# Two-layer hybrid decoder trunk on one core: openings with x normalised on ScalarE, transposes inside the output stage, and a first block whose adaptive tiles are used as they land

## The chip, the cores and the metric

The kernel runs on one core of a Trainium2 chip. The metric is the device time in microseconds (us) of one execution; lower is better. TensorE is called PE below, VectorE DVE, ScalarE ACT, GpSimd POOL, and the DMA queue that SyncE feeds SP. All data is fp32. A weight or an activation that enters a large product is first split into two fp32r parts, a high part (a rounding copy, on ACT) and a low part (the subtraction, on DVE or POOL), and a product is three matmuls.

## The reference

Each of two layers applies three sub-layers to x (512 tokens, 1024 channels): a SwiGLU FFN with half weight, a token mixer with four branches, and a second FFN. Around each sits the same frame:

```
def rmsnorm(x, g):
    y = xf * lax.rsqrt(jnp.mean(xf * xf, axis=-1, keepdims=True) + EPS)
    return (y * g.astype(jnp.float32)).astype(x.dtype)

def sandwich(x, y_fn, g_pre, g_post, shift, scale, gate, resid_w):
    h = rmsnorm(x, g_pre) * (1.0 + scale) + shift
    return x + resid_w * gate * rmsnorm(y_fn(h), g_post)

def swiglu(h, w_in, w_out):
    gate, up = jnp.split(h @ w_in, 2, axis=-1)
    return (jax.nn.silu(gate) * up) @ w_out

mod = (jax.nn.silu(c) @ w_ada[l] + b_ada[l]).reshape(B, 9, 1, D_MODEL)
```

shift, scale and gate are slices of `mod`, the "adaptive" vectors; they come from `w_ada`, 9 x 1024 x 1024 numbers a layer. The first sub-layer of layer 0 needs two of the nine slices (shift and scale) before anything else can begin.

## The kernel before, in words

**Weights** come as a stream of units of 512 KB (128 x 1024 fp32). Four slots hold them. For each unit SP loads `w_raw`, ACT makes `w_high` (`split_high`, L436), DVE makes `w_low` (`split_low`, L442), and PE uses it (`product`, L458 to L460, with the weights stationary and h moving; `token_product`, L465 to L467, in the output stage, with the activations stationary).

**Output stage** (`out_stage`, L1404). Its second half works token block by token block (tb 0 to 3, 128 tokens each): for each tb the last four units are run through, and a token block's result is complete after every 24 matmuls of 512 columns.

**Closing** (L848 on ACT, L1241 on DVE, L589 on POOL). For each tb: ACT sums the squares of y, DVE makes the mean, POOL takes the power -1/2, DVE adds y to x in two halves (L1253), ACT sums the squares of the new x (L845), DVE makes their mean (`mean_x`), and POOL makes the reciprocal root and from it a diagonal matrix `rstd_diag` (`rstd_diag`, L580).

**Opening** (L1447 on PE, L1266 on DVE, L866 on ACT). h must be channel-major. PE multiplies x by the diagonal matrix (`h_block`, L1449), which normalises and transposes at once, 8 matmuls of 128x128 for a token block, into banks 4 to 7. Then for each pair of token blocks and each of 8 channel tiles j, DVE applies scale and shift (`h_full`, L1286), ACT makes `h_high` (L873), DVE makes `h_low` (L1274). PE multiplies tile by tile into three units' banks (`products`, L1458): 8 tiles x 3 units x 3 matmuls of 256 columns for each pair. Both token blocks of pair 0 are transposed before the first product, those of pair 1 after the sixth tile of pair 0.

There are six openings: five follow an output stage, and are called boundaries below; the first has no stage before it. Before the first, SP loads the silu input, constants, 16 rows of adaptive weights in eight transfers of 1 MB (`ada_start`), three weight units after the fourth of these, then x (2 MB). DVE takes one product sum of 1024 for each of the 16 rows (L1324): eight shift rows, the low parts of three units, eight scale rows. Then `vec_scale` is made for all channels at once.

After an opening that starts an FFN, DVE increments `ada_free`; SP waits for that before it issues the silu vector, the next weight units and the adaptive tiles of the FFN, in this order in one queue. DVE needs the first adaptive tile before it completes the first FFN pair, which PE waits for after the fourth unit.

The order on each engine is the order of the code: there is no scheduler. Each engine runs its queue in order, and a wait holds all that is behind it.

## Time and profile before

| | us |
|---|---|
| median of 3 runs | 2825.34 |
| lowest, highest | 2823.95, 2826.14 |
| time of the profiled execution | 2821.51 |
| its span, first to last instruction | 2819.7 |
| PE busy | 2731.5 (97%) |
| DVE busy | 1563.4 (55%) |
| ACT busy | 1108.9 (39%) |
| POOL busy | 269.1 (10%) |

The profile was taken in one execution. 1.8 us lie around its span. PE is busy for 97% of the span, so the time outside PE's work is 88 us, and 36 us of that is the start. The mean granted TensorE clock was 0.998 of full speed.

### The profile page before, as it was taken

To read this page: it belongs to the slowest core of one execution; us is meant where nothing else is said; L and a number is where in the kernel's file an instruction comes from. 1 tells how busy PE (TensorE), PEld (TensorE's weight loads), DVE (VectorE), ACT (ScalarE), POOL (GpSimd) and SP (SyncE) were. 2 spreads that over 40 slices of the span, in tenths; PEclk is the share of its full clock that TensorE was granted. 3 is DMA by queue.
4 is the path that set the end of the run, shared out by engine and by line. 5 is a ranking of instruction groups with operands and counts; after the bars stand their busy time and mean duration, and the time that the engine had idled before them with its cause. 6 is when DMAs were issued, how large, how long until landed. Compare 5 with 4: busy or idle time off the path is not lost.

```text
span 2819.7 us, 37695 instructions
## 1 busy us (share of the span) xinstructions
PE 2731.5 (97%) x13312; PEld 2205.2 (78%) x13312; DVE 1563.4 (55%) x2636; ACT 1108.9 (39%) x2024; POOL 269.1 (10%) x360
## 2 busy tenths in 40 slices
PE   4999999999999999999999999999999999999999
PEld 4888888676777888888888888877667778888887
DVE  6655446657755657633266653565577465653323
ACT  2322234665554443222242222346665443332222
POOL 1111000111110001110011110001111000011100
PEclk9999999999999999999999999999999999999999
DMA  6655422111223325523235544221122223152331
GB/s 235 234 181 196 142 99 75 61 53 61 68 61 98 98 73 194 194 97 97 98 120 208 193 150 156 90 77 54 52 62 74 86 72 106 52 193 97 97 97 68
DMA packets 86253, 318.55 MB, mean 113 GB/s; under 512 B 9697, under 2 KB 10081, under 8 KB 84706
## 3 DMA queue, kind: packets, MB, share of 16 engines
q1 hardware_dynamic: 86114, 316.76, 33.0%
q8 instruction: 79, 1.29, 0.2%
q14 instruction: 60, 0.49, 0.1%
HBM read 314.62 MB, written 2.10 MB: 112 GB/s over the span
## 4 chain that ended last, share of the span: by engine, by line
PE 86%; DVE 6%; ACT 2%; DVEq 2%; issue 2%; DMA 2%; SPq 0%; POOL 0%; ACTq 0%; POOLq 0%
PE bank L458 19%; PE bank L460 19%; PE bank L459 19%; PE bank L465 6%; PE bank L466 6%; PE bank L467 6%; PE bank L1686 2%; PE bank L1667 2%; PE bank L1650 1%; DVE w_low L442 1%; PE bank L1658 1%; DMA ada_raw<-ada 1%; ACT w_high L436 1%; PE bank L1453 1%; DVEq L973 1%
## 5 line engine op out<-in xcount | busy, mean ns | idle before, releaser
L458 PE MATMUL bank<-h_high,w_high 128*128 128x512 f32 (+1 forms) x2528 | 974.5, 385 | 20.7 <-DVE h_low L1274 12.4
L460 PE MATMUL bank<-h_high,w_low 128*128 128x512 f32 (+1 forms) x2528 | 956.9, 379 | 0.0
L459 PE MATMUL bank<-h_low,w_high 128*128 128x512 f32 (+1 forms) x2528 | 955.3, 378 | 0.0
L442 DVE TENSOR_TENSOR w_low<-w_raw,w_high 128x1024 fp32r<-128x1024 f32 x437 | 565.7, 1296 | 634.7 <-ACT w_high L436 633.3
L436 ACT ACTIVATE w_high<-w_raw 128x1024 fp32r<-128x1024 f32 x437 | 458.5, 1051 | 357.0 <-PE bank L467 331.6
L458 PEld LDWEIGHTS bank<-h_high,w_high 128*128 128x128 f32 x2528 | 478.1, 189 | 114.2 <-issue 30.7
L460 PEld LDWEIGHTS bank<-h_high,w_low 128*128 128x128 f32 x2528 | 476.9, 189 | 90.2
L459 PEld LDWEIGHTS bank<-h_low,w_high 128*128 128x128 f32 x2528 | 477.9, 189 | 86.4 <-issue 2.4
L465 PE MATMUL bank<-w_high,ffn_high 128*128 128x512 f32 x704 | 275.6, 391 | 0.0
L467 PE MATMUL bank<-w_low,ffn_high 128*128 128x512 f32 x704 | 273.9, 389 | 0.0
L466 PE MATMUL bank<-w_high,ffn_low 128*128 128x512 f32 x704 | 273.9, 389 | 0.0
L908 ACT ACTIVATE ffn_high<-ffn_act 128x512 f32 (+1 forms) x88 | 55.7, 632 | 417.0 <-DVE ffn_act L1368 417.0
L616 POOL TENSOR_TENSOR ffn_low<-ffn_act,ffn_high 128x512 f32 x88 | 114.0, 1295 | 879.8 <-ACT ffn_high L908 879.8
L603 POOL TENSOR_TENSOR recip<-row_sum,parv 128x1 f32<-128x1 f32 x192 | 106.8, 556 | 648.1 <-ACT scores_sb L789 648.1
L1297 DVE CUSTOM_DVE_ANT_0 ada_raw<-ada_raw,silu_c 128x1024 f32<-128x1024 f32 x128 | 154.6, 1215 | 10.5 <-DMA ada_raw<-ada 10.5
L465 PEld LDWEIGHTS bank<-w_high,ffn_high 128*128 128x128 f32 x704 | 132.2, 188 | 28.4 <-issue 1.0
L466 PEld LDWEIGHTS bank<-w_high,ffn_low 128*128 128x128 f32 x704 | 132.2, 188 | 28.0 <-issue 1.0
L467 PEld LDWEIGHTS bank<-w_low,ffn_high 128*128 128x128 f32 x704 | 132.1, 188 | 27.7
L904 ACT ACTIVATE tanh_gate<-bank 128x512 f32<-128x512 f32 x88 | 52.4, 595 | 227.5 <-PE bank L460 227.5
L1368 DVE TENSOR_TENSOR ffn_act<-ffn_act,bank 128x512 f32<-128x512 f32 x88 | 60.5, 687 | 130.5 <-PE bank L460 129.1
L789 ACT ACTIVATE scores_sb<-scores_sb,neg_max 128x257 f32<-128x257 f32 (+5 forms) x192 | 101.8, 530 | 75.2 <-DVE neg_max L1157 74.5
L774 ACT ACTIVATE probs_t<-bank 128x256 f32<-128x256 f32 (+3 forms) x192 | 77.8, 405 | 133.0 <-PE bank L1667 131.9
(194 smaller groups left out, 2698.9 us busy)
## 6 DMA issues: line engine op xcount, KB each, us to landing
w_raw<-stream SPq DMA_DIRECT2D x440, 512.0 KB, 3.6
ada_raw<-ada SPq DMA_DIRECT2D x128, 512.0 KB, 3.5
ada_start<-ada SPq DMA_DIRECT2D x8, 1024.0 KB, 17.0
mixer_consts<-mixc SPq DMA_DIRECT2D x2, 1152.0 KB, 5.1
x<-x_in SPq DMA_DIRECT2D x1, 2048.0 KB, 18.8
silu_c<-silu_row SPq DMA_DIRECT2D x4, 512.0 KB, 4.3
out<-x SPq DMA_DIRECT2D x8, 256.0 KB, 2.1
lru_w<-lruw SPq DMA_DIRECT2D x2, 512.0 KB, 4.0
```

The lines of the kernel that those rows point to most:

```text
L436: eng.activation(wH[:, slot], raw[:, slot], ACT.Copy).then_inc(hi_ready[slot].sem, 1)
L442: eng.tensor_tensor(wL[:, slot], raw[:, slot], wH[:, slot].bitcast(F32), ALU.subtract).then_inc(lo_ready[slot].sem, 1)
L458: eng.matmul(o, a, rhs_h, start=first, stop=False)
L459: eng.matmul(o, a, rhs_l, start=False, stop=False)
L460: return eng.matmul(o, b, rhs_h, start=False, stop=last)
L465: eng.matmul(o, lhs_h, a, start=first, stop=False)
L466: eng.matmul(o, lhs_l, a, start=False, stop=False)
L467: return eng.matmul(o, lhs_h, b, start=False, stop=last)
L603: pool.tensor_tensor(recip[:, g % 8:g % 8 + 1], rsum[:, c:c + 1], mone, ALU.pow).then_inc(recip_ready.sem, 1)
L616: pool.tensor_tensor(fL[:, m, :], act[:, pp:pp + 1, :], fH[:, m, :].bitcast(F32), ALU.subtract).then_inc(ffn_lo.sem, 1)
L789: s.activation(s_sb[:, g % S_SLOTS, 0:w], s_sb[:, g % S_SLOTS, 0:w], ACT.Exp, scale=-1.0, bias=nmax[:, c:c + 1], accum_out=rsum[:, c:c + 1 ...
L1297: v.tensor_tensor_reduce(row, row, silu_c[:, :], 1.0, 0.0, ALU.mult, ALU.add, mod_sum[:, s:s + 1]).then_inc(ada_used.sem, 1)
```

## The change

Three things change in the five boundaries. First, normalising and transposing are separate: ACT multiplies x by the reciprocal root (`x_norm`, new L912, two activations of 512 a token block) and PE does a plain transpose against the identity. Second, the transposes of token blocks 0 and 1 stand inside the output stage, after the second of the four last units of tb 2 and of tb 3. Third, closing and opening are one function, `boundary`, in which the work of both is interleaved: on DVE the first tiles of h stand before the last token block's new x; POOL makes the low part of one weight unit (instead of DVE) and of every odd h tile.

The first opening is a function of its own. x is loaded before the adaptive tiles, whose layout is changed: for each channel tile j there is one row for the shift (a DVE product sum as before) and one 128 x 1024 tile for the scale, which PE multiplies by the silu column (`scale_row`, 8 matmuls with one moving column each). x is normalised on ACT as a whole, and PE makes products of 512 columns tile by tile as the adaptive tiles land. `ones` and `all_par` are loaded last.

```diff
-            rows = 2 * KD // ADA_GROUPS
-            for g in range(ADA_GROUPS):
-                sp.dma_start(ada_start[:, rows * g:rows * (g + 1)], ada0[:, rows * g:rows * (g + 1)]
-                             ).then_inc(ada_start_in[g].sem, 16)
-                if g == ADA_GROUPS // 2 - 1:
+            sp.dma_start(x[:, :, :], x_in).then_inc(x_loaded.sem, 16)
+            for g in range(KD):
+                sp.dma_start(ada_start[:, 2 * g:2 * g + 2], ada0[:, 2 * g:2 * g + 2]).then_inc(ada_start_in[g].sem, 16)
+                if g == 0:
                     for u in range(LEAD):
                         sp.dma_start(raw[:, u], stream[u]).then_inc(raw_full[u].sem, 16)
-                    sp.dma_start(x[:, :, :], x_in).then_inc(x_loaded.sem, 16)
             sp.dma_start(raw[:, LEAD], stream[LEAD]).then_inc(raw_full[LEAD].sem, 16)
+            sp.dma_start(ones[:, :], consts[:, P:2 * P]).then_inc(late_in.sem, 16)
+            sp.dma_start(all_par[:, :, :], pars).then_inc(late_in.sem, 16)
...
+            def boundary(l, n, u_last):            # POOL
+                for tb in range(TB - 1):
+                    rstd_y(l, n, tb)
+                    if tb < 2:
+                        rstd_x(l, n, tb)
+                split_low(pool, l, u_last + 1)
+                h_low_odd(l, n, 1)
+                rstd_x(l, n, 2)
+                h_low_odd(l, n, 3)
+                rstd_y(l, n, 3)
+                h_low_odd(l, n, 5)
+                rstd_x(l, n, 3)
+                for i in range(7, 2 * KD, 2):
+                    h_low_odd(l, n, i)
...
+            def boundary(l, n, u_last):            # ACT
+                for tb in range(TB - 1):
+                    squares_y(l, n, tb, u_last)
                     if tb == 2:
                         split_high(s, l, u_last + 1)
+                    squares_of_x(l, n, tb)
+                    if tb < 2:
+                        x_norm(l, n, tb)
+                split_high(s, l, u_last + 2)
+                h_high(l, n, 0)
+                h_high(l, n, 1)
+                split_high(s, l, u_last + 3)
+                squares_y(l, n, 3, u_last)
+                x_norm(l, n, 2)
+                h_high(l, n, 2)
+                h_high(l, n, 3)
+                squares_of_x(l, n, 3)
+                for i in range(4, KD):
+                    h_high(l, n, i)
+                x_norm(l, n, 3)
+                split_high(s, l, u_last + 4)
+                for i in range(KD, 2 * KD):
+                    h_high(l, n, i)
...
+            def boundary(l, n, u_last):            # DVE
+                for tb in range(TB - 1):
+                    new_x(l, n, tb)
+                    if tb < 2:
+                        mean_x(l, n, tb)
+                two(0)
+                split_low(v, l, u_last + 2)
+                mean_x(l, n, 2)
+                split_low(v, l, u_last + 3)
+                two(2)
                 v.drain()
+                new_x(l, n, 3)
+                two(4)
+                mean_x(l, n, 3)
+                two(6)
+                split_low(v, l, u_last + 4)
+                for i in range(KD, 2 * KD, 2):
+                    two(i)
...
+            for j in range(KD):                    # DVE, first opening
+                v.wait_ge(ada_start_in[j].sem, 16)
+                v.tensor_tensor_reduce(ada_start[:, 2 * j], ada_start[:, 2 * j], silu_start[:, :], 1.0, parv[:, j:j + 1],
+                                       ALU.mult, ALU.add, mod[:, 7 * KD + j:7 * KD + j + 1])
+                v.drain()
+                v.wait_ge(start_scale.sem, j + 1)
+                v.scalar_tensor_tensor(vecA[:, j:j + 1], bank[3][:, j:j + 1], b1[:, j:j + 1],
+                                       parv[:, 2 * KD + j:2 * KD + j + 1], ALU.add, ALU.mult).then_inc(start_vec.sem, 1)
+                if j == 1:
                     for u in range(LEAD):
+                        split_low(v, 0, u)
+                if j >= 1:
+                    start_low(j - 1)
+            start_low(KD - 1)
+            split_low(v, 0, LEAD)
...
+                    if q == units - RING + 1 and tb >= 2 and not ends(l, n):   # PE, output stage
+                        h_block(pe, l, n, tb - 2)
...
+            slots = []                                                          # PE, opening
+            for j in range(LEAD):
+                slots.append(unit_ready(pe, l, u_first + j))
+                for k in range(2):
+                    if j == 0:
+                        h_wait(0, k)
+                    unit_product(0, k, j, slots[j])
+            for k in range(2, KD - 2):
                 products(0, k)
+            h_block(pe, l, n, 2)
+            products(0, KD - 2)
+            h_block(pe, l, n, 3)
+            products(0, KD - 1)
             for k in range(KD):
                 products(1, k)
...
+            for k in range(KD):                                                 # PE, first opening
+                if k + 1 < KD:
+                    scale_row(k + 1)
+                if 4 <= k + 3 < KD:
+                    x_tile(k + 3)
+                pe.wait_ge(start_h.sem, k + 1)
```

`two(i)` on DVE writes the h tiles i and i + 1 and then the low part of tile i; POOL makes that of tile i + 1. Tile i + 1 needs the second half of the double buffer, so it waits for POOL's low part of tile i - 1 (`h_ready_odd`).

On POOL, around the last two token blocks of a boundary, the kernel before has reciprocal roots and diagonal matrices only (`wi` holds the statistics of y, `row_sum` those of x):

```order
L594 TENSOR_TENSOR wi<-wi,minus_half 128x1 [waits msy_ready]
L584 TENSOR_TENSOR row_sum<-row_sum,minus_half 128x1 [waits msx_ready]
L586 TENSOR_TENSOR rstd_diag<-ident,row_sum 128x128 [waits rsx_ready]
L594 TENSOR_TENSOR wi<-wi,minus_half 128x1 [waits msy_ready]
L584 TENSOR_TENSOR row_sum<-row_sum,minus_half 128x1 [waits msx_ready]
```

In the same place POOL now has:

```order
L607 TENSOR_TENSOR wi<-wi,minus_half 128x1 [waits msy_ready]
L458 TENSOR_TENSOR w_low<-w_raw,w_high 128x1024 [waits hi_ready2]
L620 TENSOR_TENSOR h_low<-h_full,h_high 128x256 [waits h_high_ready]
L613 TENSOR_TENSOR row_sum<-row_sum,minus_half 128x1 [waits msx_ready]
L620 TENSOR_TENSOR h_low<-h_full,h_high 128x256 [waits h_high_ready]
L607 TENSOR_TENSOR wi<-wi,minus_half 128x1 [waits msy_ready]
```

The roots of token blocks 2 and 3 now stand behind a weight split and behind low parts of h.

On DVE, from the new x of token block 2 (`y_gain`, `x`) on, the kernel before has three weight splits and the last new x before the first h tile:

```order
L442 TENSOR_TENSOR w_low<-w_raw,w_high 128x1024 [waits hi_ready2]
L442 TENSOR_TENSOR w_low<-w_raw,w_high 128x1024 [waits hi_ready3]
L442 TENSOR_TENSOR w_low<-w_raw,w_high 128x1024 [waits hi_ready0]
...
L1253 SCALAR_TENSOR_TENSOR x<-y_gain,wi,x 128x512 [waits rsy_ready]
...
L1286 TENSOR_SCALAR h_full<-bank,vec_scale,mod 128x256 [waits h_t_ready]
...
L1274 TENSOR_TENSOR h_low<-h_full,h_high 128x256 [waits h_high_ready]
```

There DVE now has (two `h_full`, one `h_low`, then two splits, two `h_full`, one `h_low`, and only then the last new x):

```order
L1358 TENSOR_SCALAR h_full<-bank,vec_scale,mod 128x256 [waits h_t_ready]
L1363 TENSOR_TENSOR h_low<-h_full,h_high 128x256 [waits h_high_ready]
L458 TENSOR_TENSOR w_low<-w_raw,w_high 128x1024 [waits hi_ready3]
...
L458 TENSOR_TENSOR w_low<-w_raw,w_high 128x1024 [waits hi_ready0]
...
L1358 TENSOR_SCALAR h_full<-bank,vec_scale,mod 128x256 [waits h_ready_odd]
...
L1340 SCALAR_TENSOR_TENSOR x<-y_gain,wi,x 128x512 [waits rsy_ready]
```

Four h tiles of pair 0 are made before the last new x, and four after it.

On PE, in the first opening, the kernel before has 16 scaled transposes and then products. PE now has, from the second adaptive tile on (`recip` is the silu column, `x_start` the normalised x):

```order
L1615 MATMUL bank<-recip,ada_start 128x1 [waits start_vectors,ada_start_in2]
L1615 MATMUL bank<-recip,ada_start 128x1 x7
L1623 MATMUL bank<-ident,x_start 128x128 [waits start_h_full]
L1623 MATMUL bank<-ident,x_start 128x128 x3
L474 MATMUL bank<-h_high,w_high 128x512 [waits start_h]
L475 MATMUL bank<-h_low,w_high 128x512
L476 MATMUL bank<-h_high,w_low 128x512
```

The scale tile k + 1 stands in PE's queue before the products of tile k.

## Rows read from the trace of the kernel before

**Rows 1.** The page's head.
```profile
span 2819.7 us, 37695 instructions
```

**Rows 2.** Waits of PE: who was waited for; total us, times, longest.
```profile
PE bank L1453 <- POOL rstd_diag L586: 35.8, 1, 35.8
PE bank L458 <- DVE h_low L1274: 12.4, 6, 2.5
PE bank L458 <- DVE ffn_act L1368: 5.3, 4, 2.2
```

**Rows 3.** Timeline of the start: start, duration, engine, line, operation [idle before].
```profile
19.17 1.06 ACT L885 ACTIVATE w_high<-w_raw 128x1024 fp32r<-128x1024 f32 x1 [12.68 <-DMA w_raw<-stream]
...
26.67 0.63 ACT L845 ACTIVATE squares_out<-x 128x512 bf16<-128x512 f32 x1 [3.88 <-DMA x<-x_in]
...
29.10 1.28 DVE L1324 CUSTOM_DVE_ANT_0 ada_start<-ada_start,silu_start,parv 128x1024 f32<-128x1024 f32 x1 [5.07 <-DMA ada_start<-ada]
...
35.75 5.81 PE L1453 MATMUL bank<-rstd_diag,x 128*128 128x128 f32 x32 [35.75 <-POOL rstd_diag L586]
...
42.71 0.36 PE L458 MATMUL bank<-h_high,w_high 128*128 128x256 f32 x1 [1.15 <-DVE h_low L1274]
```

**Rows 4.** Timeline of PE in the mixer, one-column matmuls.
```profile
446.24 2.84 PE L1511 MATMUL bank<-ones,squares 128*128 128x1 f32 x24 [1.21 <-ACT squares L718]
```

**Rows 5.** Chain of waits: start, length, what; a product of 512 columns.
```profile
406.30 0.23 PE bank L466
```

**Rows 6.** Chain of waits, in the same columns, a product in an opening.
```profile
423.06 0.12 PE bank L458
```

**Rows 7.** Chain of waits, four transposes in the mixer.
```profile
600.70 0.44 PE bank L1667 x4
```

**Rows 8.** Timeline of PE at the first boundary.
```profile
410.67 3.73 PE L1453 MATMUL bank<-rstd_diag,x 128*128 128x128 f32 x32
416.58 0.36 PE L458 MATMUL bank<-h_high,w_high 128*128 128x256 f32 x1 [2.18 <-DVE h_low L1274]
...
423.25 3.79 PE L1453 MATMUL bank<-rstd_diag,x 128*128 128x128 f32 x32
...
437.56 0.28 PE L460 MATMUL bank<-h_high,w_low 128*128 128x256 f32 x1
```

**Rows 9.** Timeline of DVE at the same boundary.
```profile
410.15 2.56 DVE L442 TENSOR_TENSOR w_low<-w_raw,w_high 128x1024 fp32r<-128x1024 f32 x2 [0.30 <-ACT w_high L436]
...
413.47 1.42 DVE L1253 SCALAR_TENSOR_TENSOR x<-y_gain,wi,x 128x512 f32<-128x512 f32 x2
414.98 0.99 DVE L1286 TENSOR_SCALAR h_full<-bank,vec_scale,mod 128x256 f32<-128x256 f32 x2
416.01 0.43 DVE L1274 TENSOR_TENSOR h_low<-h_full,h_high 128x256 fp32r<-128x256 f32 x1
...
433.24 0.43 DVE L1274 TENSOR_TENSOR h_low<-h_full,h_high 128x256 fp32r<-128x256 f32 x1
```

**Rows 10.** Timeline of ACT at the same boundary.
```profile
415.56 0.87 ACT L873 ACTIVATE h_high<-h_full 128x256 fp32r<-128x256 f32 x2
```

**Rows 11.** Timeline of POOL at the same boundary.
```profile
404.87 0.40 POOL L586 TENSOR_TENSOR rstd_diag<-ident,row_sum 128x128 f32<-128x128 f32 x1
...
410.56 1.08 POOL L586 TENSOR_TENSOR rstd_diag<-ident,row_sum 128x128 f32<-128x128 f32 x1
412.86 0.55 POOL L594 TENSOR_TENSOR wi<-wi,minus_half 128x1 f32<-128x1 f32 x1 [1.23 <-DVE wi L1246]
```

**Rows 12.** The line of POOL's subtraction of 512: ns min/median/max.
```profile
L616 POOL TENSOR_TENSOR ffn_low<-ffn_act,ffn_high x88: 1287/1296/1303, 72.2 to 2694.5; 128x512 f32 x88
```

**Rows 13.** Timeline of SP after the first opening.
```profile
59.76 0.35 SPq L527 DMA_DIRECT2D silu_c<-silu_row  x1
```

**Rows 14.** Timeline of PE, the first product after the fourth unit.
```profile
71.48 0.49 PE L458 MATMUL bank<-h_high,w_high 128*128 128x512 f32 x1 [2.24 <-DVE ffn_act L1368]
```

**Rows 15.** Busy time by windows at the third boundary: PE, PEld, DVE, ACT, POOL, granted clock.
```profile
1432.00:1436.00 4.00, 4.00 (x22) 3.91 (x21) 3.62 (x9) 1.78 (x5) 0.38 (x1) 0.57 0.00 0
```

More of the change, by code:

```diff
@@ L619, in _ @@
                         turn(i)
-                    closing(l, 2 * f)
+                    if ends(l, 2 * f):
+                        for tb in range(TB):
+                            rstd_y(l, 2 * f, tb)
+                    else:
+                        boundary(l, 2 * f, U_FFN[f] + FFN_UNITS - 1)
                     if f == 0:
@@ L1713, in _ @@
                     pe.wait_ge(pair_done.sem, pair_done.at(l, f * FT))
-                    opening(pe, l, 1 if f else -1, [u0 + j for j in range(LEAD)])
+                    if f == 1:
+                        opening(pe, l, 1, u0)
+                    elif l > 0:
+                        opening(pe, l - 1, 2, UNITS)
                     turn(0, range(LEAD, 4))
```

359 lines of the change are left out of this document (204 added, 155 removed).

## The prediction

> **What bounds the kernel now.** I read the page first: the span is 2819.7 us [rows 1] and PE is busy in 97% of it, so only PE's own work and its gaps count. The waits of PE come next [rows 2]: 35.8 us before the first matmul, 12.4 us in six waits for `h_low` (one in each opening), and 5.3 us in four waits for the first FFN pair (one after each opening that starts an FFN). Then the timeline of one boundary. With 0 as the end of the last product of the output stage (410.67), PE does 32 records of scaled transposes (3.73), idles to 5.9, does 54 products, 32 more records (3.79 with its tail, 3.55 to the next product) and 90 products, the last of which starts at 26.9; with 0.12 for it the boundary costs PE 27.0 us [rows 6, 8]. DVE finishes the last low part at 23.0 [rows 9], so `ada_free` comes 4 us before PE is through.
>
> **A boundary after the change: PE's work.** 144 products x 0.12 = 17.3 [rows 6]. A plain transpose is one record, four take 0.44 [rows 7], so 32 take 3.5; four switches between kinds at an estimated 0.1 make 3.9. Together 21.2, against 24.4 without the old waits. If nothing waited, a boundary would win 5.8 us. So the question is what waits.
>
> **The waits.** Two facts price them. POOL subtracts 512 columns in 1.296 and scales 128 in 0.40 [rows 11, 12], which by a straight line gives 0.7 for 256 and 2.45 for 1024. And POOL and DVE exclude each other: a POOL instruction that takes 0.40 alone took 1.08 when it began under a DVE subtraction at 410.56; the first of the two splits ended at about 411.38, and 0.26 later POOL was through [rows 9, 11]. So POOL work that meets a DVE subtraction waits for its end, and the other way round.
>
> Let 0 be the end of the last product of the output stage again. Token blocks 0 and 1 are normalised in time: from a finished block to `x_norm` is some 6.5 us, against 8 us and more to its transposes, so both hide. y of block 2 is finished at -6.35. Its new x ends at -3.2. POOL's weight split may begin at -3.7 but is held to -3.2 by DVE's new x, and ends at -0.8. DVE makes h tiles 0 and 1 by -2.2; ACT, which stands at the second unit's high part until -1.3, makes their high parts by -0.5; low part 0 is ready at -0.5. DVE then takes the split of unit 2 to 0.65, and POOL's low part 1 waits behind it to 1.2. PE waits 0.9 for tile 1. The third unit is split by 2.5; PE waits another 0.2 before it. The root for block 2 meets this split and ends at 2.9 (0.55 alone, [rows 11]); ACT's `x_norm` of block 2 runs to 4.1, and the high parts of tiles 2 and 3 stand behind it. With 0.42 to 0.45 for each high and low part [rows 9, 10] and 0.14 from DVE to PE (416.44 to 416.58), tile 2 reaches PE at 5.0: a wait of 1.6. Only now comes the last new x: DVE needs the product with the gain (0.7), POOL's root stands behind low part 3 and ends at 6.3, the additions take 1.42 [rows 9] to 7.7, ACT squares both halves to 8.5, and tile 4 reaches PE at 9.5, where tile 3 was through at 7.2: a wait of 2.3. Tiles 5 to 7 are in time, but block 3's `x_norm` waits until block 2's transposes have left its buffer: 0.4. After it ACT splits a unit (1.06), DVE does (1.23), and only then is tile 8 made: PE gets it at 17.75, a wait of 1.65. From there PE is the slower one (1.08 a tile against 1.8 for two on DVE and POOL) and ends at 26.4.
>
> Waits: 0.9 + 0.2 + 1.6 + 2.3 + 0.4 + 1.65 = about 7, where before they were 2.2 to 2.5. 26.4 and 2.0 for the two blocks of transposes in the output stage make 28.4, against 27.0: **1.4 slower a boundary**. Without any exclusion I get 27.2. DVE and POOL end at 23.9 + 2.0 = 25.9 instead of 23.0, so `ada_free` is 2.9 later. In all four FFN openings PE already waits for what follows `ada_free` [rows 2], so there the later of the two counts: 2.9 for the three boundaries that lead to an FFN, 1.4 for the two that lead to a mixer. Sum 3 x 2.9 + 2 x 1.4 = 11.5.
>
> **The first opening.** A 512 KB unit landed at 19.17, and x, 3 MB later, at 26.67 [rows 3]: 2.45 us a MB. x stands 2.5 MB earlier than the first unit did (4.5 MB of large transfers then, 2 MB now, issued 0.5 us sooner), so it lands at about 12.5, the adaptive tiles 0 to 7 at 14.9, 21.0 and then every 2.45 to 35.6. Squares on ACT and DVE (two blocks each, 1.3 a block) end at 15.3. POOL's power of 128x4 is not shown: above 0.55 for one column, below four times that; I take 1.4, so 17.0. `x_norm` of four times 1.0 ends at 21.0, three high parts at 24. PE's 16 transposes end at 24, scale row 1 at 26.2. DVE then makes three low parts (3.7) before low part 0: 31.0.
>
> From here PE sets the pace. Scale tile k + 1 stands before the products of tile k. One such row is 8 matmuls of fp32, two records each; 24 records of the same form (128x128 stationary, one moving column) took 2.84 [rows 4], so 16 take 1.9. They load 128x128 weights for a single column. Per tile: 1.9 for the scale row, 0.2 to DVE, 0.1 for the vector, 0.7 for the 512-column low part (between 0.43 for 256 and 1.23 for 1024), 0.14 to PE, 9 x 0.23 = 2.05 for the products [rows 5]: 5.1, the transposes lying in DVE's part. That is twice the 2.45 of a landing, so the transfers don't bound it. Six of these bring low part 6 to 61.6; after one more pair of ACT passes, the last low part is ready at 63, the fourth unit's at 64.5, `ada_free` at 64.9. The first matmuls in the old kernel ran slowly: 32 records in 5.8 where a later opening needs 3.7 [rows 3, 8], 2.1 more, a little of it perhaps for POOL's diagonals. PE is idle for 5 us before 31.0, so I charge 1.7: `ada_free` at 66.6, 6.9 later than 59.7 [rows 13]. PE resumed 11.8 after it [rows 14], and I keep that. So the first opening costs **+6.9**; from both sides, -4 if a scale row cost nothing (rival 2) and +9 if all low parts met a slow clock.
>
> **Sum.** 11.5 + 6.9 = +18.4, from 2821.5 for the profiled execution to 2840; the median of the runs lies 3.8 higher, so 2843. All other work is the same: the 1.23 that POOL takes from DVE is off PE's path, and steady loops are untouched.
>
> **The rivals.**
>
> 1. *Waits as forecast, but the clock falls too.* At the third boundary the granted clock was 0.57 over four microseconds after an idle stretch of 2.5 [rows 2, 15], between its levels of 2.4 and 1.2 GHz; that cost 0.43 x 4 = 1.7 us. In the changed boundaries PE waits five times instead of once, and the first opening has a wait in each tile. If four more boundaries fall once (6.8) and the first opening twice more (3.4), the time is 2853. Against it: at the first boundary 2.2 of idle time was followed by 54 products in 6.67 us, 0.12 each [rows 8], so no clock fell there. The Trainium skill ("TensorE: Matmul & The Clock Gate", section "HAM oscillation — how this bites in real kernels") states that matmul groups parted by waits can each start at the lower clock again. By that rule alone this rival would be likelier than the trace makes it.
>
> 2. *Faster: the waits fold into one and scale rows are cheap.* If POOL and DVE overlap more freely and ACT is never the one in front, a boundary has 21.2 + 2.2 = 23.4, which is 3.6 faster, 18 in all; if the one-column matmuls pipeline so that a row costs 0.3, a tile costs 3.4, `ada_free` comes at 56 and 4 are won. Together 2803. For it: half of the transposes' records go, and the output stage has 5 us of lead for two of four blocks. Against it: rows 4 and 11 show both costs directly. The sign turns where the waits of a boundary stay well under 5.8 and a scale row well under 1.0.
>
> 3. *No change.* The saved transposes (3.6 a boundary) are just paid back by waits (about 5.8 in all rather than 7), and the first opening gives -1 to +4, because the low parts run at full clock and x lands sooner than I say: 2822 to 2830, say 2826.
>
> **How the numbers follow.** Forecast 2843: 0.55. Rival 1, 2853: 0.16. Rival 2, 2803: 0.14. Rival 3, 2826: 0.15. 0.2% is 5.65 us, about what a measurement of this kernel tells from no change: faster means below 2819.7, slower above 2831. The forecast's own spread is 2832 to 2852 (1.5 a boundary and 3 for the start). Slower has 0.55 + 0.16 and a little of rival 3, 0.73; within, 0.13; faster, 0.14. The range 2822 to 2857 leaves out rival 2 and a slow tail, 0.14 + 0.04.
>
> **What would show it.** Right: in a boundary PE has about six gaps, of 0.9, 1.6, 2.3 and 1.65 at the tiles 1, 2, 4 and 8; POOL's 256-column subtractions take 0.7 alone and more under DVE; first products start near 31, one tile every 5.1, and SP issues the silu vector near 66. Wrong: gaps of under 4 us a boundary, scale rows of under 1 us, or `ada_free` before 60.

## The result and the profile after

The changed kernel takes 2866.24 us (2862.29 to 2867.11), where the kernel before took 2824.64 on the same chip: a ratio of 1.0141, 95% interval 1.0129 to 1.0153. The forecast was 2843. The direction was right; the loss is 41.6 us instead of 18, and lies outside the range.

First the head of the page of the changed kernel, against [rows 1].

```profile
span 2863.8 us, 37384 instructions
PE 2755.9 (96%) x13176; PEld 2215.4 (77%) x13176; DVE 1543.2 (54%) x2558; ACT 1140.9 (40%) x2057; POOL 303.1 (11%) x378
```

PE has 136 records fewer than before and is busy for longer (2755.9 against 2731.5), at a mean granted clock of 0.989 instead of 0.998. Part of the loss is thus PE running slowly, not PE waiting. Next, the waits of PE after the change, in the columns of [rows 2].

```profile
PE bank L474 <- DVE h_low L1363: 28.6, 17, 2.1
PE bank L1615 <- DMA ada_start<-ada: 14.1, 1, 14.1
PE bank L474 <- DVE ffn_act L1475: 12.5, 4, 3.9
PE bank L474 <- DVE h_low L1419: 7.8, 7, 4.3
PE bank L474 <- POOL h_low L620: 5.0, 5, 1.0
```

The start wait of 35.8 is now 14.1, but inside the boundaries 11.2 us in five waits (the 12.4 of [rows 2] less the 1.15 of the first opening) have become 28.6 and 5.0 in 22, and the four waits for `ffn_act` have grown from 5.3 to 12.5. I measured every stretch from one landmark that both kernels have, ACT's squares of token block 0 of the closing. "To PE's end" is the last 256-column product of the opening, "to SP" the issue of `silu_c`, which follows DVE's end:

| us | before | after |
|---|---|---|
| `silu_c` after the first opening | 59.76 | 72.14 |
| five boundaries, to PE's end | 43.01, 43.00, 44.81, 43.00, 43.00 | 48.57, 47.00, 46.99, 46.99, 47.34 |
| the three that lead to an FFN, to SP | 39.18, 41.00, 39.19 | 44.75, 45.06, 45.10 |

The first opening accounts for 12.4, the two boundaries into a mixer for 5.56 + 3.99, the three into an FFN for 5.57 + 4.06 + 5.91 (by SP, since PE waits there for what follows it). That is 37.5 of the 44.1 by which the span grew. The other 6.6 lie in no boundary. Over the eight microseconds around the end of each wait for `ffn_act` (from 82, 1109, 1491 and 2516) the granted clock is 0.79, where it is 1.00 in the same places before (from 70, 1087, 1461 and 2475): 4 x 8 x 0.21 = 6.7, which is about the whole of it.

**The first boundary.** PE's gaps and transposes of the changed kernel, from its timeline (start, duration, what, idle time before), against [rows 8]:

```profile
428.44 0.35 PE L474 MATMUL bank<-h_high,w_high 128*128 128x256 f32 x1 [2.13 <-DVE h_low L1363]
430.06 0.39 PE L474 MATMUL bank<-h_high,w_high 128*128 128x256 f32 x1 [1.04 <-POOL h_low L620]
433.82 0.39 PE L474 MATMUL bank<-h_high,w_high 128*128 128x256 f32 x1 [1.55 <-DVE h_low L1363]
438.14 0.39 PE L474 MATMUL bank<-h_high,w_high 128*128 128x256 f32 x1 [1.90 <-DVE h_low L1363]
...
444.41 1.09 PE L1567 MATMUL bank<-ident,x_norm 128*128 128x128 f32 x8 [0.41 <-ACT x_norm L912]
448.17 0.39 PE L474 MATMUL bank<-h_high,w_high 128*128 128x256 f32 x1 [1.60 <-DVE h_low L1363]
```

The gaps at tiles 1, 2, 4, 8 and at block 3's transposes are close to those of the forecast (0.9, 1.6, 2.3, 1.65, 0.4). The first one, 2.13 ahead of tile 0, was forecast as nothing. What is late is visible on DVE and POOL, against [rows 9, 11]; first DVE, then POOL:

```profile
422.26 3.57 DVE L1340 SCALAR_TENSOR_TENSOR x<-y_gain,wi,x 128x512 f32<-128x512 f32 x2
425.75 0.99 DVE L1358 TENSOR_SCALAR h_full<-bank,vec_scale,mod 128x256 f32<-128x256 f32 x2
427.87 0.42 DVE L1363 TENSOR_TENSOR h_low<-h_full,h_high 128x256 fp32r<-128x256 f32 x1 [1.13 <-ACT h_high L920]
```

```profile
422.54 2.73 POOL L458 TENSOR_TENSOR w_low<-w_raw,w_high 128x1024 fp32r<-128x1024 f32 x1 [0.35 <-ACT w_high L452]
428.22 1.79 POOL L620 TENSOR_TENSOR h_low<-h_full,h_high 128x256 fp32r<-128x256 f32 x1 [2.94 <-ACT h_high L920]
430.18 1.46 POOL L613 TENSOR_TENSOR row_sum<-row_sum,minus_half 128x1 f32<-128x1 f32 x1 [0.17 <-DVE row_sum L1326]
```

The two additions to x took 1.42 before [rows 9] and take 3.57 now. POOL's split arrives at 422.54, while the first addition is running; it works when that one is done (at about 422.97), and the second addition ends only 0.56 after POOL is through (425.27). So DVE held POOL back for 0.4 at most, and POOL then held DVE for 2.1. That POOL waited for the first addition shows in the first boundary of e_scale_dve (an experiment told below), where the split arrived 0.14 behind the start of the additions (399.22) instead of 0.28 behind it, took 0.13 longer and ended as long after that start, 3.0:

```profile
399.36 2.86 POOL L458 TENSOR_TENSOR w_low<-w_raw,w_high 128x1024 fp32r<-128x1024 f32 x1 [0.21 <-ACT w_high L452]
```

At 428.22 the roles are the other way round: POOL's low part, 0.73 alone, takes 1.79 under DVE's weight split.

**The first opening.** PE's first work in the changed kernel, its timeline:

```profile
14.09 3.54 PE L1615 MATMUL bank<-recip,ada_start 128*128 128x1 f32 x16 [14.09 <-DMA ada_start<-ada]
20.75 3.68 PE L1623 MATMUL bank<-ident,x_start 128*128 128x128 f32 x16 [3.11 <-ACT x_start L964]
24.21 3.41 PE L1615 MATMUL bank<-recip,ada_start 128*128 128x1 f32 x16
```

DVE's side of it, the first and third low part and the vector ahead of the third, in the same columns:

```profile
31.20 0.69 DVE L1419 TENSOR_TENSOR h_low<-norm_tmp,h_high 128x512 fp32r<-128x512 f32 x1
...
44.22 0.22 DVE L1426 SCALAR_TENSOR_TENSOR vec_scale<-bank,mod_sum,parv 128x1 f32<-128x1 f32 x1 [4.48 <-PE bank L1615]
44.35 0.68 DVE L1419 TENSOR_TENSOR h_low<-norm_tmp,h_high 128x512 fp32r<-128x512 f32 x1
```

Low part 0 starts at 31.20, as forecast (31.0). The next ones start at 37.84, 44.35, 50.87, 55.79, 60.75, 67.83 and 69.52: 6.5 to 7.1 us apart where the clock was low, 4.9 where it was full. DVE waits for PE in each, 4.5 to 5.1 in the steps at the low clock and 2.9 in those at full clock. PE stands there at the nine products of the tile before and then at its scale row. Nine products take 2.2 at full clock (51.60 to 53.78) and 3.9 at the lower one (31.94 to 35.83); a row takes 1.84 and 3.4. In this profile it was mostly the products that were slow: of the six rows in these steps one ran at the lower clock throughout:

```profile
58.73 1.84 PE L1615 MATMUL bank<-recip,ada_start 128*128 128x1 f32 x16
64.25 3.41 PE L1615 MATMUL bank<-recip,ada_start 128*128 128x1 f32 x16
```

### The profile page after: what moved, and what is told of

Its sections match the earlier page's. It is cut to its first block, busy times and chain, and to the rows that moved or that the text cites. A ratio compares the mean times of both kernels' runs of the same rounds, so it can differ in the third digit from the quotient of the medians.

```text
span 2863.8 us, 37384 instructions
## 1 busy us (share of the span) xinstructions
PE 2755.9 (96%) x13176; PEld 2215.4 (77%) x13176; DVE 1543.2 (54%) x2558; ACT 1140.9 (40%) x2057; POOL 303.1 (11%) x378
## 4 chain that ended last, share of the span: by engine, by line
PE 82%; DVE 7%; ACT 4%; issue 2%; DVEq 2%; POOL 1%; DMA 1%; ACTq 0%; SPq 0%; POOLq 0%
PE bank L474 19%; PE bank L476 19%; PE bank L475 19%; PE bank L481 6%; PE bank L482 6%; PE bank L483 6%; PE bank L1851 2%; PE bank L1832 2%; PE bank L1815 1%; DVE w_low L458 1%; PE bank L1823 1%; DVE x L1340 1%; DMA ada_raw<-ada 1%; ACT squares_out L889 1%; ACT w_high L452 1%
## 5 line engine op out<-in xcount | busy, mean ns | idle before, releaser
L474 PE MATMUL bank<-h_high,w_high 128*128 128x512 f32 (+1 forms) x2504 | 982.3, 392 | 57.2 <-DVE h_low L1363 28.6
L483 PEld LDWEIGHTS bank<-w_low,ffn_high 128*128 128x128 f32 x704 | 132.1, 188 | 27.6
```

The costliest lines, as they stand in the source:

```text
L474: eng.matmul(o, a, rhs_h, start=first, stop=False)
L483: return eng.matmul(o, lhs_h, b, start=False, stop=last)
```

## The experiments

All ratios are against the kernel before, run beside the experiment on the same chip. The medians come from several chips, on which the kernel before took 2824.0 to 2827.5, so two experiments are compared by their ratios.

**The two halves apart.** The kernel before with the changed first opening alone:

```diff
+            pe.wait_ge(consts_in.sem, 16 * 4)
+            first_opening(pe)
+            pe.wait_ge(late_in.sem, 32)
...
-                    opening(pe, l, 1 if f else -1, [u0 + j for j in range(LEAD)])
+                    if f == 1 or l > 0:
+                        opening(pe, l, 1 if f else -1, [u0 + j for j in range(LEAD)])
```

> The kernel before with the first opening of the changed one; its five boundaries are those of before. Theory (the two parts cost by themselves and add): the silu vector is issued at 72 instead of 59.8, and 1 to 2 us more are lost at the lower clock behind it, so +13 to +15 over before, 2838 to 2840. Rival (the first opening only looks late, since the layer's loads make up for it): within 4 us of before, and the boundaries carry all 42.

Measured: 2844.74, ratio 1.0058 (1.0038 to 1.0078); `silu_c` at 76.79; boundaries sum to 217.3 (216.8 before). That is above the expected 2838 to 2840: in this profile `silu_c` is 4.7 later than in the changed kernel's. Two of the six scale rows took 3.40 there instead of one, and more of the products ran at the low clock.

The changed kernel with the first opening of before (blocks of 128 x 128 scaled by the diagonal, all adaptive sums first):

```diff
-            pe.wait_ge(consts_in.sem, 16 * 4)
+            pe.wait_ge(consts_in.sem, 16 * 5)
...
-                    mm = product(pe, bank[j][:, :], slot, k * P, slice(0, P), hH[:, k], hL[:, k], k == 0, k == KD - 1)
+                    mm = product(pe, bank[j][:, cols], slot, k * P, slice(0, P), hH[:, k, cols], hL[:, k, cols], k == 0,
+                                 k == KD - 1)
```

> The changed kernel with the first opening of before; its five boundaries are the changed ones. Theory (parts add): 42 less 14, so +27 to +29, 2852 to 2854. Rival (a boundary's damage depends on what the first one leaves behind, as slots or loads out of step): under +20.

Measured: 2857.65, ratio 1.0101 (1.0077 to 1.0124); boundaries 235.1. The time is above the expected 2852 to 2854. Within the noise the halves add up: 0.58% and 1.01% make 1.59%, against 1.41% for both. The boundaries are the larger part, and both parts alone lose.

**The weight split back on DVE** (in the changed kernel):

```diff
-                split_low(pool, l, u_last + 1)
...
+                split_low(v, l, u_last + 1)
                 two(0)
```

> The changed kernel with one edit: the low part of the first unit behind a boundary is made on DVE (before the first h tiles) and not on POOL. Theory (POOL's 2.7 us subtraction takes the shared path to the SBUF before DVE's second addition to x, so this addition takes 2.8 instead of 0.7): the two additions take 1.42 again in all five boundaries, the first product behind the output stage comes about 1 to 2 us sooner each time, and the kernel is 5 to 11 us faster than the changed one, 2855 to 2861. Rival (the additions are late for POOL's root or ACT's squares, and DVE's extra 1.2 makes up for anything won): within 2 us of 2866, and the pair of additions keeps 3.5.

Measured: 2857.22, ratio 1.0119 (1.0093 to 1.0146). The pair of additions takes 1.42 again, PE's first product starts 18.12 after the landmark instead of 20.2, without a wait, and the boundaries sum to 227.5 instead of 236.9:

```profile
418.58 1.42 DVE L1339 SCALAR_TENSOR_TENSOR x<-y_gain,wi,x 128x512 f32<-128x512 f32 x2
422.65 0.36 PE L474 MATMUL bank<-h_high,w_high 128*128 128x256 f32 x1
```

A 1.23 us subtraction more on DVE, in front of tile 0, makes a boundary shorter by 1.9 us on average (3.7, 0.6, 2.1, 2.1 and 1.0). The rival is refuted: it was POOL's split alone that stretched the additions. The whole time is less clear than the trace: 9.0 us less by the medians and 6.2 by the ratios, whose intervals overlap (the four times of this kernel run from 2851.7 to 2866.5).

**Scale vectors by DVE's product sums** (in the changed kernel; the scale matrix is loaded in the layout of before):

```diff
-                v.wait_ge(start_scale.sem, j + 1)
-                v.scalar_tensor_tensor(vecA[:, j:j + 1], bank[3][:, j:j + 1], b1[:, j:j + 1],
-                                       parv[:, 2 * KD + j:2 * KD + j + 1], ALU.add, ALU.mult).then_inc(start_vec.sem, 1)
+                v.tensor_tensor_reduce(ada_start[:, 2 * j + 1], ada_start[:, 2 * j + 1], silu_start[:, :], 1.0, b1[:, j:j + 1],
+                                       ALU.mult, ALU.add, vecC[:, j:j + 1])
+                v.tensor_tensor(vecA[:, j:j + 1], vecC[:, j:j + 1], parv[:, 2 * KD + j:2 * KD + j + 1], ALU.mult
+                                ).then_inc(start_vec.sem, 1)
...
-                if k + 1 < KD:
-                    scale_row(k + 1)
```

> The changed kernel with one edit: the scale vector of the first opening is made on DVE by eight product sums of 1024 (the second row of each adaptive transfer), and the scale rows on PE are gone. Theory (the scale rows, 1.85 to 3.5 us for each of eight tiles ahead of its products, set the pace of the first opening): one tile every 3.4 to 3.7 instead of 5 to 7, the silu vector is issued at 48 to 56 instead of 72, the kernel is 14 to 24 faster than the changed one, 2842 to 2852. Rival (the chain DVE, ACT, DVE, PE between two tiles sets the pace, and PE's scale rows lie beside it): DVE's extra 1.25 a tile makes it 5 to 10 slower.

Measured: 2848.01, ratio 1.0071 (1.0050 to 1.0093), 0.70% or 20 us better than the changed kernel. `silu_c` is issued at 49.90, 22 us earlier. DVE's timeline shows the new step of a tile, 3.25 us, with no idle time in it:

```profile
29.94 1.28 DVE L1422 CUSTOM_DVE_ANT_0 ada_start<-ada_start,silu_start,parv 128x1024 f32<-128x1024 f32 x1
31.14 0.09 DVE L1422 DVE_READ_ACCUMULATOR2_ANT mod<- 128x1 f32 x1
31.14 1.28 DVE L1424 CUSTOM_DVE_ANT_0 ada_start<-ada_start,silu_start,mod_sum 128x1024 f32<-128x1024 f32 x1
32.35 0.09 DVE L1424 DVE_READ_ACCUMULATOR2_ANT vec_gate<- 128x1 f32 x1
32.51 0.16 DVE L1427 TENSOR_TENSOR vec_scale<-vec_gate,parv 128x1 f32<-128x1 f32 x1
32.59 0.69 DVE L1419 TENSOR_TENSOR h_low<-norm_tmp,h_high 128x512 fp32r<-128x512 f32 x1
```

**Both repairs in one kernel** (the last two edits together):

```diff
-                split_low(pool, l, u_last + 1)
...
-            pe.wait_ge(silu_col_ready.sem, 1)
-            scale_row(0)
```

> The changed kernel with both repairs that were measured one at a time: the scale vector by VectorE's sums (18 us less) and the weight split back on VectorE (9 us less by the sum of the boundaries). Theory (they lie in different stretches of the program and add): silu_c issued at 50, boundaries 227 to 229, time 2866 - 18 - 9 = 2839, 2835 to 2843. Rival (each repair only moves the end of one wait, and the lower clock behind the waits is paid anyway): above 2845.

Measured: 2840.87, within the expected 2835 to 2843, ratio 1.0057 (1.0042 to 1.0073); `silu_c` at 50.57, boundaries 228.2. In the traces the two add. In time the split adds 4 us by the ratios to what the scale vectors gave, which is within the noise.

**Odd low parts on DVE too**, so that POOL only takes roots in a boundary:

```diff
-                h_low_odd(l, n, 1)
...
+                    for e in (i, i + 1):
+                        pair, j = e // KD, e % KD
+                        v.wait_ge(hh_ready.sem, hh_ready.at(l, h_at(n) + e + 1))
```

> The changed kernel with the weight split before the opening and the odd low parts of h back on VectorE, so that GpSimd does only the eight powers of a boundary. Theory (a subtraction on GpSimd and VectorE's two-operand instructions keep each other waiting, and at tile 1 the low part on GpSimd is late by 1 us, but its 0.73 us instead of 0.43 on VectorE is work that VectorE is spared): the pair of x additions takes 1.42, the wait for tile 1 falls from 1.04 to about 0.5, VectorE does 8 low parts more of 0.43 = 3.4 us per boundary, of which the half behind the last wait of tile 7 ends ahead of TensorE: boundaries as in the kernel with the split alone back (227.5), within 4, time 2853 to 2860. Rival (GpSimd's part in the chain h_high to h_low is what costs): boundaries of 217 to 222, time 2842 to 2850. Rival 2 (VectorE is the limit, every us put back on it is paid): boundaries above 234, time above 2862.

Measured: 2866.09, ratio 1.0138 (1.0121 to 1.0156). This kernel keeps the scale rows on PE. The boundaries are as the theory had them (229.0, within 4 of 227.5), so POOL's low parts neither win nor lose; the time is above its range, where rival 2 had it, though rival 2's boundaries of over 234 did not come. In this profile `silu_c` comes at 75.06, where the kernel with the split alone back had 69.85 with the same code in front of it. The first opening with scale rows on PE gave 69.9, 71.2, 72.1, 74.0, 75.1 and 76.8 in six profiles, with DVE's sums 49.5 to 50.6 in six: with the rows on PE its length hangs on where the clock falls.

**Another order for ScalarE.** With both repairs and POOL out of the boundary, the high parts of tiles 2 and 3 stand ahead of `x_norm` of block 2, block 3 has its own `x_norm` buffers, and PE transposes both blocks one tile earlier:

```diff
-                x_norm(l, n, 2)
                 h_high(l, n, 2)
                 h_high(l, n, 3)
+                x_norm(l, n, 2)
                 squares_of_x(l, n, 3)
...
+                h_high(l, n, 4)
+                h_high(l, n, 5)
                 x_norm(l, n, 3)
```

> The changed kernel with the scale vector on VectorE, the weight split and the odd low parts on VectorE (as in e_no_pool), and the boundary in another order: ScalarE makes h_high 2 and 3 ahead of x_norm(2); x_norm(3) has buffers of its own (the half of post_gain that is used up, and squares_out), so that it needn't wait for the transposes of x_norm(2), and stands behind h_high 5; TensorE transposes x_norm(2) ahead of tile 5's products and x_norm(3) ahead of tile 6's. Theory (what is left of the loss in a boundary is the order of ScalarE's queue: 1.56 us at tile 2, 0.4 at each transpose block, 1.65 at tile 8, and the lower clock behind them): the waits fall to about 0.6 at tile 2 and nothing at tile 8, a boundary takes 41.5 to 43.5 instead of 45.2 to 46.7 (43.0 before), and with silu_c issued at 50 the time is 2806 to 2820. Rival (VectorE's busy time is the bound and the waits only move): boundaries stay at 45 to 46.5, time 2832 to 2842.

Measured: 2830.42, ratio 1.0019 (1.0010 to 1.0028), above the expected 2806 to 2820. The boundaries fall from 229.0 to 218.6, so the new order (ScalarE's queue, block 3's buffers and PE's transposes, moved together) was worth 10 us; the waits at tile 2 and tile 8 are 0.63 and none. But tile 4 now waits 2.1, with DVE busy 14.59 of the 16 us from 401 (windows: length, PE, PEld, DVE, ACT, POOL, clock, DMA share, GB/s):

```profile
401.00:417.00 16.00, 11.65 (x70) 9.54 (x68) 14.59 (x29) 10.29 (x23) 3.07 (x4) 0.96 0.45 172
```

The rival was right in part: its time and boundaries are too high, but up to tile 5 DVE's own work leaves hardly a gap. The boundaries take 43.4 to 44.3; one of 43.0, as before, was not reached, although by the forecast's sum a boundary without waits would be 5.8 shorter than that.

**The kernel before with the changed first opening and DVE's sums:**

```diff
+                v.tensor_tensor_reduce(ada_start[:, 2 * j + 1], ada_start[:, 2 * j + 1], silu_start[:, :], 1.0, b1[:, j:j + 1],
+                                       ALU.mult, ALU.add, vecC[:, j:j + 1])
...
+            pe.wait_ge(consts_in.sem, 16 * 4)
+            first_opening(pe)
```

> The kernel before with its five boundaries untouched and the changed first opening, in which the scale vector is made by VectorE's product sums and not by TensorE's scale rows. Theory (the parts of the change add up, and only the boundaries and the scale rows lose): the issue of silu_c comes at about 50 (59.76 before, 49.9 with the scale on VectorE in the changed kernel), the boundaries keep their 216.8 us, and the time is 2824 - 10 = 2813 to 2818, 2 to 4 us of the gain going into a wait for ffn_act of nearly 4 us and a lower clock behind it. Rival 1 (the first opening is hidden by the transfers of the adaptive matrices that follow silu_c, or paid back at the next wait): 2822 to 2826. Rival 2 (any opening that starts tiles one by one costs clock for long): over 2828.

Measured: 2817.59, ratio 0.9964 (0.9952 to 0.9976): faster than before. `silu_c` comes at 50.64, 9.1 earlier than before. PE's wait for `ffn_act` behind it is 5.15 instead of 2.24 [rows 14], which takes 2.9 of this back, and the clock behind that wait is 0.57 over four microseconds (62 to 66). The timeline of DVE shows whom PE waits for:

```profile
50.87 0.69 DVE L1408 SCALAR_TENSOR_TENSOR ffn_act<-tanh_gate,bank 128x512 f32<-128x512 f32 x1 [0.34 <-ACT tanh_gate L931]
58.34 1.23 DVE L456 TENSOR_TENSOR w_low<-w_raw,w_high 128x1024 fp32r<-128x1024 f32 x1 [6.79 <-ACT w_high L450]
59.92 1.23 DVE L1324 CUSTOM_DVE_ANT_0 ada_raw<-ada_raw,silu_c 128x1024 f32<-128x1024 f32 x1 [0.35 <-DMA ada_raw<-ada]
61.07 0.08 DVE L1324 DVE_READ_ACCUMULATOR2_ANT mod_sum<- 128x1 f32 x1
61.24 0.69 DVE L1414 TENSOR_TENSOR ffn_act<-ffn_act,bank 128x512 f32<-128x512 f32 x1
```

PE's last product before the wait starts at 56.53, so the second half of `ffn_act` needs nothing that comes after 57. It stands in DVE's queue behind a weight split and an adaptive sum, whose operands are loaded only after `silu_c` is issued. That leads to the next pair.

**`ffn_act` ahead of the adaptive sum**, in the first turn of each block:

```diff
+                            late = first and pp == 0
+                            if not late:
+                                split_low(v, l, u0 + 2 * pp + 1 + LEAD, i)
+                                steps(2 * pp + 1)
                             v.drain()
                             wait_unit(v, l, u0 + 2 * pp + 1, i)
                             v.tensor_tensor(act[:, pp], act[:, pp], bank[2 * pp + 1][:, :], ALU.mult
                                             ).then_inc(pair_done.sem, 1)
+                            if late:
+                                split_low(v, l, u0 + 2 * pp + 1 + LEAD, i)
+                                steps(2 * pp + 1)
```

In the changed kernel:

> The changed kernel, with VectorE's second half of the first activation (ffn_act, which TensorE waits for) ahead of the weight split and of the first adaptive sum in the first turn of each of the four blocks; before, it stands behind the adaptive sum, which waits for a transfer that is issued once VectorE has ended its boundary. Theory (the waits of 3.1, 2.9, 3.9 and 2.7 us for ffn_act are the late end of VectorE's boundary, handed on through silu_c and ada_raw): these waits fall to what the weight split of the next unit leaves, under 1.5 each, and with them the lower clock behind them: 6 to 11 us less, 2855 to 2860. Rival (the next weight unit arrives as late, since its transfer is issued from the same queue behind silu_c, so that TensorE only changes what it waits for): waits of 2 us and more with w_low as their cause, 2862 to 2866.

Measured: 2854.08, ratio 1.0100 (1.0085 to 1.0115): 0.41% or 11.6 us better than the changed kernel, where 6 to 11 were expected. The four waits of 12.5 us are four for `w_low` of 3.1 in all. The first is this one (PE, the same columns as above):

```profile
80.31 0.50 PE L474 MATMUL bank<-h_high,w_high 128*128 128x512 f32 x1 [0.69 <-DVE w_low L458]
```

In e_start_scale's kernel:

> The kernel before with the changed first opening, the scale vector on VectorE, and the same move of ffn_act ahead of the adaptive sum. Theory: in e_start_scale the wait for ffn_act behind the first opening is 5.15 us, and three more sum to 3.1; the weight split that TensorE needs next is done at 59.6, so the first wait shortens by 2.5, and by some 0.5 each in the others: 3 to 6 us less than e_start_scale (2817.6), 2811 to 2815. Rival (waits turn into waits for w_low, nothing gained): 2816 to 2819.

Measured: 2807.36, ratio 0.9934 (0.9920 to 0.9948), the fastest of all; 8.5 us better by the ratios and 10 by the medians than without the move, where 3 to 6 were expected.

In e_reorder's kernel:

> e_reorder (2830.4) with the same move of ffn_act as in e_act_best. Theory (a boundary of e_reorder is as long for TensorE as one of before, 218.6 against 216.8 summed, and its 11 us over e_start_scale are VectorE's end, later by 1.2 to 2.5 per boundary, handed on as waits for ffn_act of 16.0 us in all against 8.3, and the clock behind them): with the hand-over cut, 10 to 16 us less, 2814 to 2820, with waits for w_low of under 6 in all. Rival (e_reorder is slow for its boundaries and for whatever the new order does elsewhere): only the 10 us that the move gave the other opening, or less, 2820 to 2826.

Measured: 2813.44, ratio 0.9955 (0.9943 to 0.9967), 17 us better than e_reorder by the medians and 18 by the ratios. Its boundaries are as before the move (219.6). Of the 13 us by the medians (15.5 by the ratios) that e_reorder had lost against e_start_scale, 6 are left against e_act_best; the rest fits DVE's later end (41.7 and 42.1 us to SP against 39.2 and 40.9), handed on.

**Filling PE's gaps.** Products of the identity with itself, read by nobody:

```diff
+                if pair == 0:
+                    fill(pe, bank[0][:, 256:384], {2: 6, 4: 8, 7: 6}.get(k, 0))
...
                     turn(0, range(LEAD, 4))
+                    fill(pe, bank[4][:, 0:P], 11, True)
```

> The changed kernel with products of the identity matrix that nothing reads put in TensorE's waits: 4, 6, 8 and 6 of 128 columns ahead of tiles 1, 2, 4 and 7 of each boundary, and 11 behind the first turn of each block, ahead of the wait for ffn_act. No wait of another engine changes. Theory (some 6.6 us of the loss are TensorE at its lower clock behind waits of 3 to 4 us, and 2 more in the boundaries): the clock stays at 1.00 after these waits, mean clock 0.993 or more, 4 to 9 us less than the changed kernel, 2857 to 2862. Rival (the clock is lower for another reason than the idle time, or the waits end no sooner since VectorE sets them): the same time within 2, 2864 to 2868; or the fillers are late themselves and add: above 2868.

Measured: 2862.60, ratio 1.0120 (1.0105 to 1.0136). The interval still touches that of the changed kernel, so the gain of 4 to 6 us is not certain, and the mean clock is 0.990 in this profile, not 0.993. What is certain is the clock behind the waits for `ffn_act`. The window behind the first wait for `ffn_act`, first of the changed kernel, then of this one (columns as above):

```profile
83.00:87.00 4.00, 3.36 (x8) 2.69 (x9) 2.36 (x3) 3.01 (x4) 1.28 (x1) 0.57 0.74 270
```

```profile
83.00:87.00 4.00, 3.32 (x21) 2.80 (x20) 2.26 (x4) 2.19 (x4) 1.31 (x1) 1.00 0.64 215
```

The granted clock stays at its upper level (2.4 GHz) where PE had something to do, and is at its lower one (1.2 GHz) for most of the window where PE had idled for 3.1. It stays at 1.00 behind the three other waits too (from 1108, 1491 and 2517; 0.86, 0.77 and 0.57 in the changed kernel). The fillers inside the boundaries gained nothing (236.5 against 236.9): in the first boundary the clock then fell earlier (0.74 from 428 to 432), behind the first gap of 2.13, which had no filler.

## Why the prediction was wrong, point by point

**What bounds the kernel.** Right: the loss lies in PE's waits and in its own speed.

**PE's work in a boundary, and the waits at tiles 2, 4 and 8.** Right: 1.55, 1.90 and 1.60 for 1.6, 2.3 and 1.65; 0.41 for 0.4; 1.04 for the 0.9 and 0.2 at tile 1 and the third unit. With the split back on DVE three of the five boundaries take 44.9, 1.9 more than the 43.0 of four boundaries before, where the forecast had 1.4.

**"POOL's weight split may begin at -3.7 but is held to -3.2 by DVE's new x, and ends at -0.8": this is the step that failed.** The arrival was good (0 lies at 426.15, so 422.54 is -3.6), and so was the rule that the two exclude each other. The split never ran alone; its 2.70 to 2.73 hold up to 0.4 of waiting, so the estimated 2.45 fits. What failed is how far DVE's new x was, and with it who waits. In the forecast the new x ends at -3.2, and the split meets its second addition. But ACT's `x_norm` of block 1 (419.27 to 420.61) stands ahead of the squares of y of block 2, which start 0.9 behind the last product of that block instead of 0.2. At -3.2 only the first addition was done. The split came in between DVE's two additions, and the second one waited for POOL. So tile 0 was late by 2.13 instead of 0. The rows from which the rule was taken show such a case, and I had not used it: at 410.56 POOL also worked between two splits of DVE, and DVE's second one waited. The two took 2.56 there [rows 9], while three in a row took 3.49 at 27.80 of the changed kernel, 1.13 apart. e_split_dve takes this away and gets 1.9 us a boundary back, about 9 in all by the traces.

The Trainium skill ("GPSIMD Engine Reference", section "Key points") says that GpSimd shares its SBUF interfaces with VectorE and that it contends with VectorE's instructions that have two SBUF inputs. By that rule the trace agrees: the stretched instruction has two such inputs, and `h_full`, which reads PSUM, passed beside POOL's low part later in the boundary, both as long as alone (POOL, then DVE):

```profile
448.19 0.73 POOL L620 TENSOR_TENSOR h_low<-h_full,h_high 128x256 fp32r<-128x256 f32 x1 [6.93 <-ACT h_high L920]
448.21 0.54 DVE L1358 TENSOR_SCALAR h_full<-bank,vec_scale,mod 128x256 f32<-128x256 f32 x1
```

In each case here it was the one that came second that waited: DVE at 422.97, and again with two instructions of one column (0.57 at 433.87 and 0.68 at 438.23, 0.16 alone), POOL at 428.22.

**"If four more boundaries fall once": rival 1 was half of the truth.** I gave the lower clock 0.16 on the ground of one boundary where 54 products ran at full speed after a wait of 2.2. The clock fell in every boundary of the changed kernel. In the first it fell at 438.5, after four waits: the products stand 0.21 apart there, 0.12 before. In the other four it fell earlier, behind the wait at tile 0 and about the wait at tile 1 (0.73, 0.55, 0.68 and 0.63 over four microseconds from 20 us after the landmark). There it cost little, for these boundaries take 47.0 to 47.3 and the first takes 48.6. With 2.1 for POOL and that 1.6, 1.4 becomes 5.1 of the 5.56 measured; in the second mixer boundary 1.4 + 2.1 makes 3.5 of 3.99. Rival 1 did not name a place where much of it was lost, the stretches behind the four waits for `ffn_act`: the clock is 0.79 over eight microseconds at each, which makes 6.7 us, about the 6.6 that lie in no boundary. The Trainium skill ("TensorE: Matmul & The Clock Gate", section "HAM oscillation — how this bites in real kernels") has matmul groups parted by waits start at the lower clock again. By that rule, rival 1 should have had more than 0.16, and the traces of the changed kernel and of e_fill_bound bear it out.

**DVE's end, "+2.9 for the three boundaries that lead to an FFN".** The rule was right, that there the later of the two ends counts, and the size was off mainly for the same reasons: 5.57, 4.06 and 5.91. That DVE needs an adaptive tile before it completes the first pair stands in the description of the kernel before; that this is only the order of DVE's queue and can be taken away I had not seen. e_act_after and e_reorder_act show it.

**The first opening, "+6.9".** x landed at 11.5 (12.5), low part 0 began at 31.2 (31.0), a scale row takes 1.84 (1.9) and a tile 4.95 (5.1) at full clock. The charge of 1.7 for the slow clock was the error: six steps took 36.6 us instead of 30.6. The mechanism was right, the clock term mis-sized by some 4.3; another 0.2 comes before low part 0 and 1.0 after low part 6. Against six steps at full clock (4.95 each) these lost 6.9, of which some 4.8 are products and 2.1 scale rows. That low part 0 came on time is partly luck: scale row 1 ended at 27.6 and not at 26.2, and 26.2 with 3.7 behind it makes 29.9, not 31.0. The measured end of 72.1 is 12.4 late, beyond the +9 that I took for the worst case and had not worked out from PE's products and rows at the slow clock. e_scale_dve shows what the row on PE was worth, with the slow clock that came with it: 22 us to `silu_c`.

**Rivals 2 and 3** fell. Rival 2's turning point was right: a step without PE's row (3.25, near its 3.4) makes the first opening win, as e_start_scale shows, 9 us to `silu_c`.

In sum: of the 25.7 us between 18.4 and 44.1, 10.5 are POOL's split (5 x 2.1; 9.4 by e_split_dve's boundaries), 5.5 the first opening, 6.6 the clock behind the waits for `ffn_act`. The remaining 3 are a difference that no run takes apart; 1.6 of them are the clock in the first boundary.

What is open: why the clock falls in one boundary of the old form and not in its twin (43.0 or 44.4 in the same code), and whether the fillers shorten the whole at all.

## What to carry to other kernels

Before moving an operation to GpSimd, look at what VectorE does with two SBUF operands just then, and price it with GpSimd arriving first: the move of 1.23 us off VectorE cost about 2 us on the path in each boundary. A chain in which TensorE does a small step between waits (here 16 one-column records and nine products a tile) should be priced at its lower clock, products and all, and if another engine has the time, the step moved there. When a boundary ends later on an engine that isn't the bound, follow the first instruction behind it that needs a transfer, and see who stands in the queue after it: one reordered instruction was worth 8 to 18 us in three kernels.

## What the hardware showed beyond this

- GpSimd's root over 128x4 took 1.92 us, against 0.55 for 128x1 [rows 11]; the forecast had taken 1.4. Its subtraction of 128x256 took 0.73 alone.

```profile
14.47 1.92 POOL L648 TENSOR_TENSOR row_sum<-row_sum,minus_half 128x4 f32<-128x4 f32 x1 [13.59 <-DVE row_sum L1414]
```

- At the start the granted clock is shown as 1.00 from 14 to 35, yet PE's records there are as long as at the lower level: 16 one-column records took 3.54 at 14.09 and 3.41 at 24.21, 1.84 later. In the kernel before, 32 records took 5.81 from 35.75 [rows 3] at a shown clock of 1.00, and 3.73 later [rows 8]. So in these profiles the clock's column says nothing ahead of PE's first dense work; there the length of the records has to be read.
